# Differential attention maps weighed in two passes instead of four, a reordered ScalarE queue, and the last attention moved into the block before it

## The reference

```python
# even layer: sparse latent attention (8 heads, top-k keys) beside a differential attention (4 heads)
p = safe_softmax(s, causal)                      # s: two score maps for each of 4 heads
a = p[:, :, 0] - lam_full * p[:, :, 1]
o = einsum('bhqs,bshe->bqhe', a, v)              # v and o are 128 wide for each head
o = rmsnorm(o, subln_gain) * (1.0 - lam_init)    # o / sqrt(mean(o*o) + eps) * gain

# odd layer: sum of three attentions under sigmoid gates g, 16 heads in 4 groups
return g0 * o_cmp + g1 * o_slc + g2 * o_win      # compressed, selected and window keys
```

## Time and profile before

| | us |
|---|---|
| median of 3 runs | 1092.57 |
| profiled execution, its own time | 1092.25 |
| its span in the trace | 1090.5 |
| even attention, first score to the low half of the differential output | 517.43 to 560.80 |
| last instruction of `odd_in` to first matmul of `sparse_attention` | 822.68 to 824.51 |
| sparse attention, first score to the projection behind it | 824.51 to 891.35 |
| TensorE busy | 984.1 (90% of the span) |

### The profile page before, as it was taken

How to read it: one execution, slowest core, us unless ns; L and a number is a source line. 1 busy time by engine, 2 the same in 40 slices (tenths; PEclk the granted TensorE clock), 3 DMA queues, 4 the chain that set the end, 5 groups by cost and what they waited for, 6 DMA issues and landing times. The chain is left out here.

```text
span 1090.5 us, 20488 instructions
## 1 busy us (share of the span) xinstructions
PE 984.1 (90%) x8701; PEld 702.3 (64%) x8701; DVE 593.2 (54%) x970; ACT 478.8 (44%) x821; POOL 94.4 (9%) x105
## 2 busy tenths in 40 slices
PE   6998899879766776999999999999998999999997
PEld 5675788544333332788558777776985548777774
DVE  5656788440000001799856644554986866645543
ACT  5556562310000002774655553354665656534532
POOL 3410370000000000106010000000030000000000
PEclk9899999879888889999999999999998999999999
DMA  8834004999999998773323756664634022776521
GB/s 252 257 118 132 2 3 176 423 398 420 421 421 421 421 422 294 250 238 119 114 82 118 248 180 226 230 194 155 208 109 155 2 88 88 231 231 224 179 99 39
DMA packets 108747, 228.68 MB, mean 210 GB/s; under 512 B 7305, under 2 KB 86203, under 8 KB 94075
## 3 DMA queue, kind: packets, MB, share of 16 engines
q1 hardware_dynamic: 105691, 219.38, 55.5%
q0 software_dynamic: 2976, 8.14, 2.6%
HBM read 224.63 MB, written 1.05 MB: 207 GB/s over the span
## 5 line engine op out<-in xcount | busy, mean ns | idle before, releaser
L906 PE MATMUL later_pB<-field 128*128 128x256 f16 x1920 | 212.9, 273 | 0.0
L906 PEld LDWEIGHTS later_pB<-field 128*128 128x128 f16 x1920 | 187.8, 98 | 25.5
L735 DVE SCALAR_TENSOR_TENSOR field<-field 128x2048 f16<-128x2048 f32 x84 | 153.8, 1869 | 57.1 <-ACT field L630 57.1
L630 ACT ACTIVATE field<-field 128x2048 f16<-128x2048 f32 x84 | 126.4, 1567 | 15.8 <-DMA field<-in_ffn_w_up 9.6
L915 PE MATMUL later_pB<-field 128*128 128x512 f16 x528 | 117.7, 379 | 0.6 <-DVE field L735 0.6
L366 PE MATMUL later_pB<-field 128*128 128x256 f16 (+2 forms) x960 | 115.2, 274 | 1.1 <-ACT field L305 0.3
L366 PEld LDWEIGHTS later_pB<-field 128*128 128x128 f16 x960 | 94.1, 98 | 14.7 <-ACT field L305 1.8
L1383 PE MATMUL rw_pB<-ring,kept 128*32 128x256 f32 x864 | 70.0, 419 | 23.4 <-DMA ring<-in_w_up 20.4
L915 PEld LDWEIGHTS later_pB<-field 128*128 128x128 f16 x528 | 51.5, 98 | 58.9 <-issue 1.5
L1316 DVE TENSOR_TENSOR rw_mu_a<-rw_pB,rw_mu_a 128x256 f32<-128x256 f32 x8 | 3.4, 424 | 122.7 <-PE rw_pB L1383 122.7
L1383 PEld LDWEIGHTS rw_pB<-ring,kept 128*32 128x32 f32 x864 | 38.0, 121 | 48.3 <-issue 34.6
(11 more groups left out here) (586 smaller groups left out, 1577.2 us busy)
## 6 DMA issues: line engine op xcount, KB each, us to landing
ring<-in_w_gate SPq DMA_DIRECT2D x27, 1024.0 KB, 26.1
ring<-in_w_up SPq DMA_DIRECT2D x27, 1024.0 KB, 26.7
ring<-in_w_down SPq DMA_DIRECT2D x24, 1024.0 KB, 26.2
field<-in_ffn_w_down SPq DMA_DIRECT2D x22, 1024.0 KB, 5.0
field<-in_ffn_w_gate SPq DMA_DIRECT2D x20, 1024.0 KB, 7.4
field<-in_ffn_w_up SPq DMA_DIRECT2D x20, 1024.0 KB, 9.7
wt<-in_ev_w_in SPq DMA_DIRECT2D x9, 1024.0 KB, 6.0
wt<-in_od_w_in SPq DMA_DIRECT2D x9, 1024.0 KB, 5.6
```

The costliest lines, as they stand in the source:

```text
L630: copy = lambda o, i, scale=1.0: nc.scalar.activation(o, i, ACT.Copy, scale=scale)
L735: return nc.vector.scalar_tensor_tensor(out, whole, scale, hi, ALU.mult, ALU.subtract)
L906: ins = T.matmul(p[:, s, j * SEQ:(j + 1) * SEQ], w[:, s, m, c, j::NJ], h[:, c, :], start=(n == 0), stop=(n == 3 * KC - 1))
```

## The change

1. In a differential unit the first map stays as the exponentials left it. Its sum goes to a tile of its own, `own_sums`; the second map's factor becomes minus lambda times the first sum over the second, so the unit's result is the old one times its first sum. The norm divides that out, with eps multiplied by the squared sum.
2. On ACT the copies of a unit stand before the exponentials of unit u + 2; the first heads' copies `high(2)`, `high(3)` and the squares stand at u = 4 instead of 5.
3. On DVE half of one `take_eight` moves ahead of `smallest(0)`; at u = 5 `weigh(6)` stands before `smallest(7)`, not behind it.
4. On TensorE the second to fourth groups of unread matmuls go from 8, 3, 3 to 2, 2, 2, and a group of 4 is put before the wait for `picked`.
5. `sparse_attention` and its feed-forward join the block of the rest. POOL clears only the semaphores of `even_in` and `even_attention`, behind its last work, and raises `cleared`; each other engine waits for `cleared` and then for the semaphores of what it reads. The compressed scores stand between `score(0)` and `score(1)` on TensorE. The load of the last feed-forward's second block waits for two scores.

```diff
@@ even_attention, scalar
+                    total = own_sums[:, u, t:t + 1] if is_diff(u) and i == 0 else den[:, u % 2, i, t:t + 1]
                     ins = nc.scalar.activation(E[...], pS[...], ACT.Exp, bias=..., scale=-1.0,
-                                               accum_out=den[:, u % 2, i, t:t + 1])
+                                               accum_out=total)
...
         for u in range(units):
-            if u + 2 < units:
-                exps(u + 2)
-            if u >= 2:
-                high(u - 2)
             if is_diff(u):
                 left_of_one(u)
             else:
                 right(u)
-            if u == 5:
+            if u + 2 < units:
+                exps(u + 2)
+            if u >= 2 and u != 5:
+                high(u - 2)
+            if u == 4:
+                high(3)
                 act.wait_ge(high_out, 4)
                 nc.scalar.activation(sq[:], dT[:], ACT.Square, scale=P ** -0.5).then_inc(squared, 1)
@@ even_attention, vector, weigh(u)
-            link(nc.vector.reciprocal(part[:, at], den[:, at]))
             if is_diff(u):
-                link(nc.vector.tensor_scalar(part[:, at, 1], part[:, at, 1], neg[:, 0:1], None, ALU.mult))
...
+                link(nc.vector.reciprocal(part[:, at, 1], den[:, at, 1]))
+                link(nc.vector.scalar_tensor_tensor(part[:, at, 1], part[:, at, 1], neg[:, 0:1], own_sums[:, u],
+                                                    ALU.mult, ALU.mult))
                 for t, c0, nk in SPAN:
+                    whole, less = E[:, at, 0, c0:c0 + nk], E[:, at, 1, c0:c0 + nk]
+                    ins = nc.vector.scalar_tensor_tensor(whole, less, part[:, at, 1, t:t + 1], whole, ALU.mult, ALU.add)
@@ even_attention, vector
+        take_eight(pick, SPAN[0:1])
         smallest(0)
...
         smallest(1)
-        take_eight(pick)
+        take_eight(pick, SPAN[1:2])
         weigh(0)
         for u in range(units):
+            if u == 5:
+                weigh(6)
             if u + 2 < units:
                 smallest(u + 2)
-            if u + 1 < units:
+            if u + 1 < units and u != 5:
                 weigh(u + 1)
...
             if u == 6:
+                link(nc.vector.tensor_tensor(st[:, 2, :], sums, sums, ALU.mult))
                 dve.wait_ge(squares_summed, 1)
-                link(nc.vector.tensor_scalar(st[:, 0, :], pS[:, 0, 0, 0:8], EPS, None, ALU.add))
+                link(nc.vector.scalar_tensor_tensor(st[:, 0, :], st[:, 2, :], EPS, pS[:, 0, 0, 0:8], ALU.mult, ALU.add))
@@ even_attention, tensor
             if u + 2 == 4:
+                unread(4)
                 pe.wait_ge(picked, 1)
             if u + 2 < units:
                 score(u + 2)
-            if u == 0:
-                unread(8)
-            if u in (1, 2):
-                unread(3)
+            if u in (0, 1, 2):
+                unread(2)
@@ sparse_attention
+        wait_alone(sp, begun, cleared, 1)
+        sp.wait_ge(tiles_split, len(ODD_TILES))
...
+        wait_alone(act, begun, cleared, 1)
+        act.wait_ge(moved, len(ODD_TILES))
+        act.wait_ge(kw_roped, 1)
         nc.scalar.activation(gates[:], y[:, :, 2560:2608], ACT.Exp, scale=-1.0).then_inc(gate_exps, 1)
...
+        wait_alone(dve, begun, cleared, 1)
...
+        wait_alone(pe, begun, cleared, 1)
+        pe.wait_ge(ks_out, 1)
+        pe.wait_ge(moved, len(ODD_TILES) - 1)
         score(0)
-        score(1)
         for n in range(PAIRS):
...                                                    # compressed scores
         ins.then_inc(c_scored, 1)
+        pe.wait_ge(kw_out, 2)
+        pe.wait_ge(moved, len(ODD_TILES))
+        score(1)
@@ hybrid_kernel
+                gone = held.take_back(("in2", "ea"))
...
+                    @block.gpsimd
+                    def _(pool):
+                        in2_pool(pool)
+                        in3_pool(pool)
+                        nc.clear_and_free_semaphores(gone)
+                        pool.sem_inc(cleared, 1)
+                        last_layer()
...
-            with Held(nc) as held, ExitStack() as ctx3:
...
-                with nc.Block(no_gpsimd_drain=True) as block:
```

More of the change, by code:

```diff
@@ L3343, in weigh @@
             at = u % 2
-            link(nc.vector.reciprocal(part[:, at], den[:, at]))
             if is_diff(u):
-                link(nc.vector.tensor_scalar(part[:, at, 1], part[:, at, 1], neg[:, 0:1], None, ALU.mult))
-            for i in range(2):
+                link(nc.vector.reciprocal(part[:, at, 1], den[:, at, 1]))
+                link(nc.vector.scalar_tensor_tensor(part[:, at, 1], part[:, at, 1], neg[:, 0:1], own_sums[:, u],
+                                                    ALU.mult, ALU.mult))
                 for t, c0, nk in SPAN:
[L3349 to L3356, removed]
+                    whole, less = E[:, at, 0, c0:c0 + nk], E[:, at, 1, c0:c0 + nk]
+                    ins = nc.vector.scalar_tensor_tensor(whole, less, part[:, at, 1, t:t + 1], whole, ALU.mult, ALU.add)
+            else:
+                link(nc.vector.reciprocal(part[:, at], den[:, at]))
+                for i in range(2):
+                    for t, c0, nk in SPAN:
+                        own = E[:, at, i, c0:c0 + nk]
+                        ins = nc.vector.tensor_scalar(own, own, part[:, at, i, t:t + 1], None, ALU.mult)
             ins.then_inc(weighed, 1)
@@ L3759, with sparse_attention @@
 NSA_NAMES = ["scored", "least", "exped", "weighed", "probs_turned", "probs_left", "probs_right", "summed", "high_out", "low_out",
-             "c_scored", "c_masked", "c_less", "c_exped", "c_weighed", "c_turned", "c_out", "gate_exps", "vlink"]
-def sparse_attention(nc, ctx, sems, con, y, o, low, outT, room, pB, project_first, start):
+             "c_scored", "c_masked", "c_less", "c_exped", "c_weighed", "c_turned", "c_out", "gate_exps", "vlink", "begun"]
+def sparse_attention(nc, ctx, sems, con, y, o, low, outT, out, room, pB, made, cleared, project_first, start):
     per_group = PAIRS // C_G
@@ L3990, in tensor @@
             if u == units - 2:
+                pe.wait_ge(out.low, KC)
                 project(0)
@@ L4129, in hybrid_kernel, with last_layer @@
                 odd_weights.take(odd_out_sems, [odd_wide.take([P, D]) for _ in range(2)] + [odd_inner.take([P, D]) for _ in range(2)])
-                with nc.Block(no_gpsimd_drain=True) as block:
+                cleared, = held.take("cleared", ["cleared"])
+                gone = held.take_back(("in2", "ea"))
+                odd_side = dict(zip(ODD_SIDE, in3_sems))
+                last = {}
+                def last_layer():
+                    nsa_sems, ffn_sems = held.take("nsa", NSA_NAMES), held.take("ffn3", FFN_NAMES + LAST_NAMES)
+                    nsa_sem = lambda n: nsa_sems[NSA_NAMES.index(n)]
+                    ffn_rooms = {"w_up32": region(A_), "wu": region(B_), "late": region(L_)}
+                    last["ffn"], project_first = feed_forward(nc, ctx2, ffn_sems, "ffn3", con, oT, odd_weights, ffn_rooms, pB, wt, arrived_of["out3"], 0,
+                                                              *ffn_of(1), x, mix, Freed((nsa_sem("scored"), 2), (nsa_sem("low_out"), PAIRS)),
+                                                              last=(a["norm_final_2"], tokens(out[0])))
+                    nsa_room = Room(field[:, edges[L_] + odd_room.at:edges[L_ + 1]])
+                    made = (pr_odd.lo_ready, pr_odd.moved, *(odd_side[n] for n in ("q_out", "ks_out", "kw_out", "kw_roped")))
+                    last["nsa"] = sparse_attention(nc, ctx2, nsa_sems, con, y_odd, o, low, oT, odd_weights, nsa_room, pB, made, cleared,
+                                                   project_first, start=block_loads("out3", 1))
+                with nc.Block(no_gpsimd_drain=True) as block:
+                    @block.gpsimd
[5 more added lines that the diff above has]
+                        last_layer()
                     @block.sync
@@ L4136, in _ @@
                         in3.sync(sp)
[L4138 to L4141 removed]
+                        last["nsa"].sync(sp)
+                        last["ffn"].sync(sp)
                     @block.scalar
@@ L4148, in _ @@
                         in3.scalar(act)
+                        last["nsa"].scalar(act)
+                        last["ffn"].scalar(act)
                     @block.vector
```

63 lines of the change are left out of this document (23 added, 40 removed).

## The result

| | before | after |
|---|---|---|
| median | 1094.22 us (1089.83 to 1101.55, 20 runs) | 1087.02 us (1084.25 to 1092.62, 20 runs) |
| ratio of the runs, 95% interval | | 0.9936 [0.9921, 0.9951] |
| profiled execution: span | 1090.5 | 1082.9 |

The change makes the kernel 7.0 us faster (0.64%, interval 5.4 to 8.6). The forecast was 3.4. Against the three runs shown ahead (1092.57) the median is 5.6 less, and against the longer series of 20 it is 7.2 less.

The account below looks back on a forecast made before the run. TensorE was taken as the bound, with DVE pacing key choice and early sparse attention. Even attention -3.4, boundary -0.4 and end +0.4 made -3.4 us on 1092.25, 1088.9; the figure given was 1089.0, range 1085.4 to 1092.0.

Parts of the forecast that it names:

- Up to `score(4)`: Even attention, DVE choosing keys: score(4) starts 1.87 us earlier, 0.71 from half a take_eight and 1.16 from weigh.
- From there to `turn(4)`: Even attention, TensorE: one unread matmul fewer 0.27 us, copies first remove the 0.45 us wait; running gain 2.59.
- the rival of the exponentials: Even attention, ACT: later exponential groups become the bound, 4 waits of 0.5 us take 2 back: 1091; chance 0.14 with the merge failing.
- `turn(6)`: Even attention, decided by DVE's weigh(6) and left(5): TensorE starts it 3.3 us earlier, about 1.4 of the 2.02 wait left.
- Squares a unit sooner: Even attention, ACT: squares move under score(7) and turn(5), summing directly follows turn(6); counted 0.1 us.
- The low stretch: Even attention behind turn(6), 549 to 553: TensorE's clock at 0.62 of full lost 1.5 us; assumed to remain.
- The three cases: Even attention's gain: 3.4 us with the clock as before, 4.9 without a low stretch, 1.9 with a second like it.
- its case with the clock up: Low stretches in even attention (1.5 us) and sparse attention (1.4) both vanish: sum -6.3, 1086.2 us; chance 0.14.
- The boundary: Before sparse attention: TensorE's gap goes but DVE waits for score(1), so 0.4 us gained; rival 1086.9 us, chance 0.08.
- the prediction's bound with `score(1)` at half clock: Start of sparse attention: score(1) takes twice as long, DVE 0.8 us later than before, a loss of about 0.8.
- a sign of being wrong: Sparse attention: the prediction called itself wrong if, among other signs, compressed_scores starts 1 us or more earlier.
- The end: Kernel's end: one clear of 133 semaphores, 78 more at 5.4 ns each, adds 0.42 us; about 0.75 us in all.

Follow-up runs that it names:

- squares_late: Changed kernel with the third and fourth head's copy and the squares back at u = 5, behind right(5) and exps(7): 1090.64 us, 0.9958 of before.
- warm: Changed kernel with both sparse scores ahead of the compressed ones and unread matmuls in both stages' TensorE waits, run twice: 1083.95 and 1083.74 us, 0.9902 and 0.9886 of before.
- before_warm: Kernel before the change with 8 unread matmuls in TensorE's wait at turn(6) of even attention: 1093.06 us, 0.9994 of before.
- scores_first: Changed kernel with both of sparse attention's scores ahead of the compressed ones, as before the change: 1084.52 us, 0.9918 of before.
- unread_back: Changed kernel with even attention's unread matmuls back at 8, 3, 3 and none ahead of the wait for picked: 1087.55 us, 0.9932 of before.
- even_only: Kernel before with only the even attention edits (with take_eight); sparse attention stays in its own block: 1090.07 us, 0.9948 of before.

## Why the prediction was right and where it wasn't

The median lies in the range (1085.4 to 1092.0) and the sign is right. The figure itself, 1089.0, was 2.0 too high: it forecast 3.4 us (0.31%), 7.0 (0.64%) came, and the likeliest case, less than 0.5%, wasn't the one that came. (By its own sum the figure should read 1089.2: 1088.9 and 0.3.) In even attention most steps came out as forecast; the median's place in the range is partly the clock's doing and partly unexplained.

- **Up to `score(4)`**: 1.93 us, forecast 1.87. The rows have both terms: DVE's idle time ahead of `smallest(0)` went from 0.96 to 0.23 us, and from the start of `weigh(0)` to the next `smallest` it is 1.12 instead of 1.72 us. Neither was run by itself.
- **From there to `turn(4)`**: it comes 3.05 sooner (19.32 behind the first score instead of 22.37), forecast 2.59. The wait of 0.45 us is gone as forecast. What the prediction left out is the wait of 0.19 us ahead of `turn(2)`, for ACT's copy of the unit before; it is gone too. The unread matmul fewer is worth 0.38, not 0.27. Between `score(4)` and `turn(6)` TensorE has no other wait, so the rival of the exponentials is out.
- **`turn(6)`**: 3.72 sooner, forecast 3.3; the wait left is 1.32, forecast 1.4, and DVE's `left(5)` ends it, as forecast. Right. But the prediction credited the copies with 0.45 us. They are worth 1.58 in the old kernel and 2.31 in the new one. The walk had `turn(6)` as DVE's and so had their effect inside the 3.3; it named only the wrong part as its cause. What `weigh(6)` ahead of `smallest(7)` brings on DVE was not run by itself.
- **Squares a unit sooner, "I count 0.1"**: as a term of the sum it is right. The sums follow `turn(6)` by 0.69 us instead of 0.85, so 0.16 more, and start 3.88 sooner (forecast 3.4). As the price of the edit it is far off: by squares_late the sums come 1.92 us later without it, 1.75 of it TensorE's waiting. The prediction counted from before's place of the squares, where they ended just before the sums, not from where they would stand once `turn(6)` is 3.7 us sooner.
- **The low stretch, "1.5, left in"**: the old even attention took 43.32 to 43.37 us in three profiles (in one with unread matmuls added), each with a clock loss of 1.7. The new one took 37.76 and 37.75 where the loss was 0, and 41.00 twice where it was 3.4. A loss of 1.7 it never had; with the 12.99 us that followed the sums at that loss in the old kernel and in squares_late it would be 39.5, an estimate, so 3.9 us at equal clock where 3.4 was forecast. The stage gives 5.6 with the clock up (forecast 4.9) and 2.4 with a loss of 3.4 (forecast 1.9). The three cases were the right list and the clock's price was near (3.2 us between the outer two, forecast 3.0); all three are 0.5 to 0.7 low, 0.5 of it from the terms above. The even half of its case with the clock up, given 0.14, happened in two of four profiles of this code (and in both of warm). The Trainium skill, "TensorE: Matmul & The Clock Gate", Part 4 (PE-mode transpose), says that transposes don't count as busy time for the clock in the way that matmuls do. before_warm agrees so far that matmuls put ahead of the six transposes didn't stop the fall behind them; but the same transposes and sums ran at full clock in after and scores_first, and that transposes are the cause no run here shows.
- **The boundary, 0.4**: the mechanism was right (the gap gone, DVE waiting 4.17 us for `score(1)`, forecast over 3). In the first profile `compressed_scores` came 9.96 us after the transposes, the prediction's bound with `score(1)` at half clock; in the second 8.64, 0.6 better than before, and 8.14 in unread_back, where both scores and the small matmuls ran at full clock. The last is 1.1 sooner than before, past the 1 us that the prediction named as a sign of being wrong: its walk had the small matmuls at 4.34, as a falling clock had left them, and they took 3.76 there. By the stage, at like clock loss the merge gives 0.9 us at 3.4 (60.16 and 59.24), between -0.1 and 0.4 at 1.7 (58.64 against 58.72 and 58.22), and at 5 to 7 it gives 0.2 and 1.6 (61.23 against 61.06 and 59.59, these two with more loss than before's). Over all profiles it is 59.7 on average in six with the merge and 61.5 in four without it; but 1.4 of these 1.8 us come from one profile, even_only's 65.78 with a loss of 10.2. What the merge brings is not sized by these runs.
- **The end, +0.42**: +0.64 in every merged kernel (207.92 to 208.00 against 207.25 to 207.31). The two clears take 0.79 us together, where the forecast had one of 0.75; the second clear's drain came with it and was missed.

Even attention at 5.6 or 2.4 (4.0 on average), the boundary's average of 1.8 and the end's -0.64 make 5.1 us of the 7.0, and the interval begins at 5.4. What is over isn't explained. The start of even attention varied from 513.3 to 519.0 over the profiles, with the expert layer's loads ahead of it; kernels with the even change had it at 516.5 on average and the four others at 517.9. Whether that is chance stays open. So does what makes the clock fall in one execution of the same instructions and not in the next: the two profiles of the changed kernel, with one code and one wait of 1.32 us, lost 0 and 3.4 us. The Trainium skill, "TensorE: Matmul & The Clock Gate", Part 1, says that the chip judges activity on a beat that is free-running and doesn't begin with the kernel; that would make it a matter of where in the beat the stage falls. The runs agree so far that equal code had both; none of them moves the stage on purpose.

## What to carry to other kernels

On an engine with one list, a short copy that another engine waits for goes ahead of a long group that itself waits for a third: the copy costs the group half a microsecond, the reverse order cost 2.3. When several edits shorten one chain, the price of the later ones has to be taken from where the earlier ones leave it: the copies alone brought the sums 0.96 us, while in the changed kernel undoing the copies costs them 2.30 us and undoing the squares 1.92. So two such edits can't be priced by adding up what each brings alone. And where a stage can run at two clocks, forecast it at each and give both. Compare kernels at a point ahead of the low stretch, where equal code agreed within 0.02 us here, and take more than one profile before a stage's length is believed.

## What the runs showed of the hardware that was not expected

Low stretches in even attention came in two sizes only, a loss of 1.7 us (four of thirteen profiles) or 3.4 (five), or not at all (four); in the start of sparse attention the loss went from 1.7 to 10.2 us, for kernels whose instructions there differ little. What followed the sums in even attention took 11.3, 13.0 or 14.5 us by the size of the stretch, whatever edit stood ahead of it. At half clock a score (8 matmuls of 64 rows by 128 columns) took 1.65 us instead of 0.93, the six transposes 1.54 instead of 0.87, and the 32 small matmuls 7.03 instead of 3.76. The kernels with two range clears at the end, each with a drain ahead of it, took 0.64 us longer there than those with one.
